# The projections' weight tiles loaded from ScalarE's queue instead of the sync engine's

## The chip, the cores and the metric

One Trainium2 chip; the kernel runs on 1 core. The metric is the device time of a run in microseconds (us). The kernel before has a median of 1959.77 us over 3 runs (1958.41 to 1960.76). The execution that was profiled took 1963.19 us, with a span of 1961.4 us from the first to the last instruction of the program.

## The reference

One layer of a hybrid decoder, on 1024 tokens of width 1024, float32, with 16 learned tokens put in front:

```
proj = rmsnorm(h) @ w_in                       # 1024 -> 10256 columns, split in 12 parts
q, k, v = silu(causal conv, 4 taps, of gq, gk, gv);  q, k normalised per head
o_a = gated delta rule over 8 heads of 128, in chunks (a triangular solve in each chunk)
o_b = retention over 4 heads of 256, in chunks, on rotated rq, rk and on rv
y = sigmoid(gate_a) * rms(o_a) * silu(gz) + sigmoid(gate_b) * silu(rg) * rms(o_b)
h = h + y @ w_out
h = h + (silu(a) * b) @ w_down,   a, b = split(causal conv, 3 taps, of rmsnorm(h) @ w_up)
out = rmsnorm(h), without the 16 tokens
```

## The kernel before

**Number format.** Each large product is made of three passes. An operand x is kept as x_hi (rounded to the matmul's fast format) and x_lo = x - x_hi, and the product is w_hi·x_hi + w_hi·x_lo + w_lo·x_hi.

**Tiles and units.** The first projection is made from 80 weight tiles of 1024 x 128 (tile t = 0 to 79; 512 KB each). Each tile is worked off in three *units* (t, 0), (t, 1), (t, 2): one third of the columns of the sequence, 24 matmuls into one PSUM bank. Units are numbered u = 3t + j and alternate between PSUM banks 0 and 1. The eight tiles of `w_out` (80 to 87) and the first six of `w_up` follow; the rest of the feed-forward block uses another scheme of tiles.

**What happens to a weight tile.** (1) A DMA loads it to the staging buffer `w_raw` (a few tiles go to a part of `ext`). (2) ScalarE (ACT) copies `w_raw` to `w_hi` (`split_high`, L1549). (3) VectorE (DVE) computes `w_lo = w_raw - w_hi` (`split_low`, L1936) and raises the semaphore `w_lo`. (4) TensorE (PE) uses both. `w_raw` is one buffer, so that the DMA of tile t+2 can only be issued when step 3 of tile t+1 is done. `w_hi` and `w_lo` have two buffers each, used by tiles in turn.

**What happens to a unit.** PE raises `units_done`. ACT copies the PSUM bank to the buffer `raw` (L1624, called the *evacuation* of the unit below) and raises `evac`. Unit u starts only when `evac` has reached u-1, that is when unit u-2, which used the same bank, has been evacuated (L1170: `pe.wait_ge(evac, ... u - 1)`).

**The order of work.** `front_plan()` makes one list of steps. Each engine's program walks the whole list and issues, for each step, its own part; an engine works strictly in that order, and waits on semaphores where a step needs another engine. The order in which an engine meets the steps is thus the order of the plan. The steps that matter here, in the order around a unit (t, 0):

- `("proj", t, 0)`: PE's 24 matmuls; on ACT the evacuation of that unit.
- `("split", t+1)`: `w_hi` of tile t+1 on ACT, `w_lo` of it on DVE.
- `("load", t+2)`: the DMA of tile t+2 into `w_raw`. Its wait is for `w_lo` of tile t+1. (In the stretch of the retention value tiles 24 to 31, a table `loads_at` places the loads one by one.) There are 79 of these steps, for tiles 3 to 81.
- `("proj", t, 1)`: the next unit, and its evacuation on ACT.

Between them the plan puts the steps of the recurrent parts: `conv` (L2044, L2048 on DVE) and `silu` (L1683 on ACT) for the delta rule's q, k, v tiles; `r_sc`, `r_out`, `r_ss` for a chunk of the retention (`r_ss`: Ln and Exp on ACT at L1696 and L1698, then the scaled output on DVE at L2103, which PE's next `r_out` at L1258 needs, since it reuses the banks); `dec`, `dec_e` (two Exp on ACT, L1723 and L1725), `qk` (L2168 on DVE, L2666 on GpSimd) for a chunk of the delta rule. Functions of ACT of different kinds need another table (`ACT_TABLE_LOAD`, L1533).

**The queues.** The sync engine (SP) issues nearly all DMAs of the kernel, in plan order: weight loads, stores of the rotated and convolved tiles to scratch in HBM (`store`, L806; `store_turned`, L813 and L815), and the loads of the chunks. ACT issues none before the change. GpSimd (POOL) issues the sums of the down projection's weights: four DMAs of 2816 KB at the end of tile 4, and small ones later. The loads from tile 82 on are issued by SP at L1034.

Of the kernel before, what the change touches and what calls it, by code (L numbers as in the profile page):

```python
# [60 lines left out]
T_ROT, T_K, T_RV, T_Q, T_V, T_ZB, T_ZA, T_END = 0, 16, 24, 32, 40, 48, 64, 80  # L61
# [357 lines left out]
def program(nc, io, sc, out):  # L419

    with ExitStack() as ctx:
# [10 lines left out]
        def sem(name):  # L432
            return ctx.enter_context(nc.semaphore("f1_" + name))
# [97 lines left out]
        def erow(at, n=1024):  # L531
            return tile8(ext[:, at:at + n])
# [4 lines left out]
        def wr(t):  # L537
            return (erow(4096) if t in (1, T_RV, T_RV + 2) else erow(5120) if t in (2, T_RV + 1) else w_raw[:, :, :])

        def w_seen(t):  # L540
            if t in (1, T_RV, T_RV + 2):
                return w_in[1], 16 * (1, T_RV, T_RV + 2).index(t) + 16
            if t in (2, T_RV + 1):
                return w_in[2], 16 * (2, T_RV + 1).index(t) + 16
            return w_in[0], 16 * (1 if t == 0 else t - 1 if t < T_RV else t - 4)

        def w_parts(t):
# [43 lines left out]
        w_hi, w_lo, units_done, evac, pe_x15 = (sem(n) for n in (  # L591
            "w_hi", "w_lo", "units_done", "evac", "pe_x15"))
# [139 lines left out]
        def weights_of(t):  # L732
            if t in (T_RV + 4, T_RV + 5):

                return io["w_in"][T_RV + 4 + t % 2]
            return io["w_in"][t] if t < T_END else io["w_out"][t - T_END] if t < T_UP else io["w_up"][t - T_UP]
# [62 lines left out]
        def _(sp):  # L799
# [22 lines left out]
            for step in plan:  # L822
                kind, a = step[0], step[1:]
                if kind == "intro":
# [15 lines left out]
                    sp.dma_start(sc["kt"][0, 0:PAD, :], zero[0:PAD, :]).then_inc(zero_done, 16)  # L840
                    for n in ("rvt", "rkt"):
                        sp.dma_start(sc[n][0, 0:PAD, :], zero[0:PAD, :]).then_inc(zero_done, 16)
                elif kind == "load":
                    t = a[0]
                    sp.wait_ge(w_lo, 1 if t == 3 else 3 if t in (T_RV, T_RV + 1) else T_RV + 1 if t == T_RV + 2 else
                               T_RV if t == T_RV + 3 else t)
                    sp.dma_start(wr(t), weights_of(t)).then_inc(w_seen(t)[0], 16)
                elif kind == "rope":
                    i = a[0]
                    store(0, S_RQ + 2 * i, d_rope, 6 * i + 4)  # L850
# [18 lines left out]
                elif kind == "silu":  # L869
                    t = a[0]  # L870
# [657 lines left out]
        def _(act):  # L1528
# [28 lines left out]
            for step in plan:  # L1557
                kind, a = step[0], step[1:]
# [33 lines left out]
                elif kind == "proj":  # L1592
                    t, j = a
# [31 lines left out]
                elif kind == "proj3":  # L1625
                    t = a[0]
# [20 lines left out]
                elif kind == "ab":  # L1647
                    table(LNEXP)
                    turned = psum[:, 7, 0:NCH * 2 * GH].rearrange("p (c g) -> p c g", c=NCH)
                    if a[0] == 0:  # L1650
                        act.wait_ge(ab_step, 1)
                        act.activation(gtmp[:, :, GH:2 * GH], turned[:, :, GH:2 * GH], ACT.Exp,
                                       scale=-1.0).then_inc(ab_step, 1)
                        act.activation(gabs[:, :, :], gtmp[:, :, 0:GH], ACT.Abs).then_inc(ab_step, 1)
                        act.wait_ge(ab_step, 3)
                        act.activation(gabs[:, :, :], gabs[:, :, :], ACT.Exp, scale=-1.0).then_inc(ab_step, 1)
                        act.wait_ge(ab_step, 4)
                        act.activation(gabs[:, :, :], gabs[:, :, :], ACT.Ln, bias=1.0).then_inc(ab_step, 1)
                        act.activation(rate[:, :], arow[:, 0, :], ACT.Exp).then_inc(ab_step, 1)
                    elif a[0] == 1:  # L1660
                        act.wait_ge(ab_step, 14)
                        act.activation(gates[:, :, NBEG], gcum[:, :].rearrange("p (c g) -> p c g", c=NCH),
                                       ACT.Exp).then_inc(ab_step, 1)
                        act.activation(gates[:, :, EGL], psum[:, 7, 216:288].rearrange("p (c g) -> p c g", c=NCH),
                                       ACT.Exp).then_inc(ab_step, 1)
                        act.activation(gates[:, :, KDEC], gates[:, :, KDEC], ACT.Exp).then_inc(ab_step, 1)
                    else:
                        act.wait_ge(pe_ab, 3)
                        act.activation(grows[:, :], psum[0:NCH * GH, 7, 288:416], ACT.Copy).then_inc(rows_out, 1)
                elif kind == "silu":  # L1670
                    t = a[0]
                    q = convs_before(t)
# [1094 lines left out]
```

## Time and profile before

| | |
|---|---|
| median of 3 runs | 1959.77 us |
| profiled execution, its span | 1963.19 us, 1961.4 us |
| PE busy | 1932.7 us (99%) |
| DVE busy | 1286.9 us (66%) |
| ACT busy | 795.8 us (41%) |
| POOL busy | 330.5 us (17%) |
| DMA, mean rate | 161 GB/s |

The profile page shows one execution. Busy time is that of computing instructions; issuing a DMA does not count as busy. In a timeline each row is an instruction (or several of one kind in a row): start, duration, engine, source line, operation, output <- inputs, shape, count, and in brackets the idle time of the engine before it with what ended it. SPq is the sync engine's own stream, in which the row of a DMA is only its issue.

### The profile page before, as it was taken

To read this page: it belongs to the slowest core of one execution; us is meant where nothing else is said; L and a number is where in the kernel's file an instruction comes from. 1 tells how busy PE (TensorE), PEld (TensorE's weight loads), DVE (VectorE), ACT (ScalarE), POOL (GpSimd) and SP (SyncE) were. 2 spreads that over 40 slices of the span, in tenths; PEclk is the share of its full clock that TensorE was granted. 3 is DMA by queue.
4 is the path that set the end of the run, shared out by engine and by line. 5 is a ranking of instruction groups with operands and counts; after the bars stand their busy time and mean duration, and the time that the engine had idled before them with its cause. 6 is when DMAs were issued, how large, how long until landed. Compare 5 with 4: busy or idle time off the path is not lost.

```text
span 1961.4 us, 32138 instructions
## 1 busy us (share of the span) xinstructions
PE 1932.7 (99%) x13173; PEld 1865.5 (95%) x13173; DVE 1286.9 (66%) x1612; ACT 795.8 (41%) x1094; POOL 330.5 (17%) x327
## 2 busy tenths in 40 slices
PE   8999999999999999999999999999999999999998
PEld 7999997999999999999999999999999999988887
DVE  6456764747676766676643333379988889866666
ACT  5223432534333444444443333334444444445443
POOL 0000002566573122222101101200000000000001
PEclk9999999999999999999999999999999999999999
DMA  9666567654555676555445642322433545577564
GB/s 293 219 206 140 129 168 189 200 174 152 171 184 140 155 201 171 160 143 170 147 119 171 177 122 82 100 84 63 132 88 117 152 151 162 153 254 264 191 191 161
DMA packets 301222, 315.99 MB, mean 161 GB/s; under 512 B 151004, under 2 KB 221124, under 8 KB 300948
## 3 DMA queue, kind: packets, MB, share of 16 engines
q1 hardware_dynamic: 291860, 290.86, 48.0%
q0 software_dynamic: 9216, 23.07, 5.9%
q8 instruction: 105, 1.72, 0.4%
q14 instruction: 41, 0.34, 0.1%
HBM read 222.76 MB, written 114.18 MB: 172 GB/s over the span
## 4 chain that ended last, share of the span: by engine, by line
PE 91%; DVE 4%; DMA 2%; ACT 1%; issue 1%; POOL 1%; SPq 0%; DVEq 0%; ACTq 0%; POOLq 0%
PE a_psum L1174 36%; PE a_psum L1469 18%; PE a_psum L155 10%; PE a_psum L1479 10%; PE a_psum L1161 5%; PE a_psum L1261 1%; PE a_psum L1280 1%; PE a_psum L1258 1%; PE a_psum L1366 1%; PE a_psum L1290 1%; PE a_psum L1350 1%; PE a_psum L1306 1%; PE a_psum L1381 1%; PE a_psum L1243 1%; PE a_psum L1389 1%
## 5 line engine op out<-in xcount | busy, mean ns | idle before, releaser
L1174 PE MATMUL a_psum<-xh,w_hi 128*128 128x342 f32 (+3 forms) x1632 | 528.6, 324 | 3.6 <-DVE w_lo L1936 3.6
L1174 PE MATMUL a_psum<-xl,w_hi 128*128 128x342 f32 (+3 forms) x1632 | 523.3, 321 | 0.0
L1174 PE MATMUL a_psum<-xh,w_lo 128*128 128x342 f32 (+3 forms) x1632 | 521.4, 319 | 0.0
L1174 PEld LDWEIGHTS a_psum<-xh,w_hi 128*128 128x128 f32 x1632 | 307.2, 188 | 6.2 <-DVE w_lo L1936 4.2
L1174 PEld LDWEIGHTS a_psum<-xl,w_hi 128*128 128x128 f32 x1632 | 307.4, 188 | 0.8
L1174 PEld LDWEIGHTS a_psum<-xh,w_lo 128*128 128x128 f32 x1632 | 307.1, 188 | 0.0
L1624 ACT ACTIVATE post<-a_psum 128x342 f32<-128x342 f32 (+3 forms) x204 | 93.1, 457 | 488.7 <-PE a_psum L1174 461.4
L1936 DVE TENSOR_TENSOR w_lo<-w_raw,w_hi 128x1024 fp32r<-128x1024 f32 x86 | 112.8, 1312 | 132.7 <-ACT w_hi L1549 132.7
L1549 ACT ACTIVATE w_hi<-w_raw 128x1024 fp32r<-128x1024 f32 x86 | 90.5, 1053 | 102.0 <-PE a_psum L155 74.7
L1479 PE MATMUL a_psum<-act_hi,down_hi 128*128 128x512 f32 (+1 forms) x324 | 124.0, 383 | 2.8 <-DVE act_lo L2477 2.7
L1469 PE MATMUL a_psum<-x_t_hi,up_hi 128*128 128x258 f32 x608 | 123.3, 284 | 2.7 <-DVE post L2424 2.5
L1479 PE MATMUL a_psum<-act_hi,down_lo 128*128 128x512 f32 (+1 forms) x324 | 124.2, 383 | 0.0
L1479 PE MATMUL a_psum<-act_lo,down_hi 128*128 128x512 f32 (+1 forms) x324 | 123.9, 382 | 0.0
L1469 PE MATMUL a_psum<-x_part_lo,up_hi 128*128 128x258 f32 x608 | 122.7, 283 | 0.0
L2356 DVE SCALAR_TENSOR_TENSOR post<-post,c_par,post 128x1024 f32<-128x1024 f32 x88 | 111.2, 1282 | 2.4 <-ACT post L1823 0.6
L2048 DVE SCALAR_TENSOR_TENSOR post<-post,a_par,post 128x1040 f32<-128x1040 f32 x72 | 97.0, 1347 | 2.6
L1469 PEld LDWEIGHTS a_psum<-x_t_hi,up_hi 128*128 128x128 f32 x608 | 95.0, 191 | 3.2 <-issue 2.9
L1469 PEld LDWEIGHTS a_psum<-x_part_lo,up_hi 128*128 128x128 f32 x608 | 94.0, 189 | 0.0
L2576 POOL DMA_DIRECT2D down_sums<-down_sums x22 | 17.9, 814 | 449.7 <-DVE post L2362 449.7
L1469 PE MATMUL a_psum<-x_t_lo,up_hi 128*128 128x258 f32 x456 | 92.8, 285 | 0.0
L1469 PE MATMUL a_psum<-x_b_hi,up_hi 128*128 128x258 f32 x456 | 91.8, 283 | 0.5 <-DVE u_three L2422 0.5
L1469 PE MATMUL a_psum<-x_t_hi,up_sum_lo 128*128 128x258 f32 x456 | 92.0, 283 | 0.0
(294 smaller groups left out, 3964.4 us busy)
## 6 DMA issues: line engine op xcount, KB each, us to landing
w_raw<-in_w_in SPq DMA_DIRECT2D x75, 512.0 KB, 3.9
up_raw<-in_w_up SPq DMA_DIRECT2D x19, 1024.0 KB, 4.9
mix_scratch<-post SPq DMA_DIRECT2D x32, 522.0 KB, 2.9
down_sums<-in_w_ffn_down POOLq DMA_DIRECT2D x4, 2816.0 KB, 31.1
act_scratch<-post SPq DMA_DIRECT2D x22, 512.0 KB, 2.7
down_raw<-down_sums SPq DMA_DIRECT2D x44, 256.0 KB, 2.7
act_raw<-act_sums SPq DMA_DIRECT2D x44, 256.0 KB, 3.1
ext<-mix_scratch SPq DMA_DIRECT2D x9, 1024.0 KB, 7.3
```

Source lines behind the costliest of these rows:

```text
L155: mm = pe.matmul(psum[:, bank + j, 0:n], w[:, k, :], x[:, k, col + n * j:col + n * j + n], start=(k == 0 and part == 0), stop=(k == KC - 1 ...
L1161: mm = pe.matmul(psum[0:rows_, u % 2, n * i:n * i + n], x[:, k, x0:x0 + rows_], w, start=(k == 0 and part == 0), stop=(k == KC - 1 and par ...
L1174: mm = pe.matmul(psum[:, u % 2, 0:n], w[:, k, :], x[:, k, at0:at0 + n], start=(k == 0 and part == 0), stop=(k == KC - 1 and part == 2))
L1243: mm = pe.matmul(four(7)[:, h, seen(c)], r_in[:, 8 + 2 * h + e, :], r_in[:, 2 * h + e, seen(c)], start=(e == 0), stop=(e == 1))
L1258: mm = pe.matmul(o, rvs[c % 2][:, n, :], rsc[:, h, seen(c)], start=True, stop=(c == 0))
L1469: mm = pe.matmul(region(i, n)[:, b, :], w[:, k, :], x[:, k, HP * b:HP * b + HP], start=(n < 4 and k == 0 and part == 0), stop=(k == 3 and ...
L1479: mm = pe.matmul(psum[:, (0, 4, 0, 4, 0, 4, 0)[p] + m, c0:c0 + n], a, b[:, c0:c0 + n], start=(p not in (2, 5, 6) and k == 0 and part == 0) ...
L1549: act.activation(w_parts(t)[0], wr(t), ACT.Copy).then_inc(w_hi, 1)
L1624: act.activation(dst, src, ACT.Copy).then_inc(evac, 1)
L1936: dve.tensor_tensor(lo, wr(t), hi.bitcast(F32), ALU.subtract).then_inc(w_lo, 1)
L2048: dve.scalar_tensor_tensor(out=acc[:, 0:n], in0=x, scalar=w, in1=acc[:, 0:n], op0=ALU.mult, op1=ALU.add).then_inc(d_conv, 1)
L2356: dve.scalar_tensor_tensor(out=acc_of(j, s), in0=u_out[s][:, c0:c0 + SEQ], scalar=par2[:, at0:at0 + 1], in1=acc_of(j, s), op0=ALU.mult, op ...
```

## The change

The branch for the step `load` is taken out of SP's program and put into ACT's, word for word except for the engine: the same plan, the same wait, the same source, destination and semaphore. The 79 loads of tiles 3 to 81 are thus issued by ACT; tiles 0 to 2 and those from 82 on stay with SP.

```
@@ sync engine @@
-                elif kind == "load":
-                    t = a[0]
-                    sp.wait_ge(w_lo, 1 if t == 3 else 3 if t in (T_RV, T_RV + 1) else T_RV + 1 if t == T_RV + 2 else
-                               T_RV if t == T_RV + 3 else t)
-                    sp.dma_start(wr(t), weights_of(t)).then_inc(w_seen(t)[0], 16)
@@ ScalarE @@
+                elif kind == "load":
+                    t = a[0]
+                    act.wait_ge(w_lo, 1 if t == 3 else 3 if t in (T_RV, T_RV + 1) else T_RV + 1 if t == T_RV + 2 else
+                                T_RV if t == T_RV + 3 else t)
+                    act.dma_start(wr(t), weights_of(t)).then_inc(w_seen(t)[0], 16)
```

## Rows read from the trace of the kernel before

**Rows 1.** The page's first part: busy time, share and instructions of each engine.
```profile
PE 1932.7 (99%) x13173; PEld 1865.5 (95%) x13173; DVE 1286.9 (66%) x1612; ACT 795.8 (41%) x1094; POOL 330.5 (17%) x327
```

**Rows 2.** Waits of PE: who waited for whom, us in total, times, longest.
```profile
PE a_psum L1174 <- DVE w_lo L1936: 3.6, 2, 2.1
```

**Rows 3.** Waits of the sync engine's stream, same columns.
```profile
SPq L847 <- DVE w_lo L1936: 311.7, 53, 15.0
```

**Rows 4.** Tile `w_raw`: durations min/median/max in ns; the page's POOL DMAs (mean 814 ns).
```profile
L847 SPq DMA_DIRECT2D w_raw<-in_w_in x74: 328/333/1416, 35.6 to 1152.5; - x74
DMA to landing us min/median/max: 3.4/3.9/12.8
...
L2576 POOL DMA_DIRECT2D down_sums<-down_sums x22 | 17.9, 814 | 449.7 <-DVE post L2362 449.7
```

**Rows 5.** Timeline of ACT and DVE, 1048 to 1053 us, a regular stretch.
```profile
1048.06 0.46 ACT L1624 ACTIVATE post<-a_psum 128x342 f32<-128x342 f32 x1 [1.26 <-PE a_psum L1174]
...
1051.83 0.46 ACT L1624 ACTIVATE post<-a_psum 128x342 f32<-128x342 f32 x1 [2.36 <-PE a_psum L1174]
...
1050.95 1.22 DVE L1936 TENSOR_TENSOR w_lo<-w_raw,w_hi 128x1024 fp32r<-128x1024 f32 x1
```

**Rows 6.** Timeline of ACT, DVE and PE, 646 to 653 us.
```profile
646.16 1.07 ACT L1683 ACTIVATE post<-post 128x1040 f32<-128x1040 f32 x1 [3.00 <-DVE post L2048]
...
649.27 0.63 ACT L1698 ACTIVATE y<-y 128x512 f32<-128x512 f32 x1
...
646.04 1.22 DVE L1936 TENSOR_TENSOR w_lo<-w_raw,w_hi 128x1024 fp32r<-128x1024 f32 x1
...
649.93 1.22 DVE L2103 TENSOR_TENSOR y<-a_psum,y 128x1024 f32<-128x1024 f32 x1 [0.88 <-ACT y L1698]
...
652.36 0.38 PE L1258 MATMUL a_psum<-ext,y 128*128 128x128 f32 x2
```

**Rows 7.** Timeline of ACT, DVE and PE, 686 to 697 us.
```profile
686.85 0.46 ACT L1624 ACTIVATE post<-a_psum 128x346 f32<-128x346 f32 x1 [0.70 <-PE a_psum L1174]
687.33 1.28 ACT L1533 ACT_TABLE_LOAD   x1
691.51 1.07 ACT L1683 ACTIVATE post<-post 128x1040 f32<-128x1040 f32 x1 [2.90 <-DVE post L2048]
...
696.01 0.44 ACT L1624 ACTIVATE post<-a_psum 128x346 f32<-128x346 f32 x1
...
691.39 1.22 DVE L1936 TENSOR_TENSOR w_lo<-w_raw,w_hi 128x1024 fp32r<-128x1024 f32 x1
...
692.66 0.43 PE L1174 MATMUL a_psum<-xh,w_hi 128*128 128x342 f32 x1 [2.06 <-DVE w_lo L1936]
...
696.55 0.37 PE L1174 MATMUL a_psum<-xh,w_hi 128*128 128x342 f32 x1
```

**Rows 8.** Timeline of ACT, DVE and POOL, 673 to 687 us.
```profile
673.63 0.46 ACT L1624 ACTIVATE post<-a_psum 128x346 f32<-128x346 f32 x1 [2.40 <-PE a_psum L1174]
...
679.00 1.06 ACT L1723 ACTIVATE y<-y 128x1024 f32<-128x1024 f32 x1 [1.23 <-DVE y L2158]
...
674.32 1.22 DVE L1936 TENSOR_TENSOR w_lo<-w_raw,w_hi 128x1024 fp32r<-128x1024 f32 x1
...
681.36 1.29 DVE L2168 TENSOR_TENSOR y<-a_psum,y 128x512 f32<-128x512 f32 x2 [1.13 <-ACT y L1725]
...
684.05 3.41 DVE L2044 TENSOR_SCALAR post<-post,a_par 128x1040 f32<-128x1040 f32 x1
...
684.05 2.39 POOL L2666 TENSOR_TENSOR y<-y 128x1024 f32<-128x1024 f32 x1 [0.17 <-POOL post L2662]
```

**Rows 9.** Timeline of ACT and PE, 104 to 107 us; the page's DMA issues.
```profile
104.01 1.06 ACT L1549 ACTIVATE w_hi<-w_raw 128x1024 fp32r<-128x1024 f32 x1 [6.20 <-DMA w_raw<-in_w_in]
...
106.38 0.43 PE L1174 MATMUL a_psum<-xh,w_hi 128*128 128x348 f32 x1 [1.52 <-DVE w_lo L1936]
...
down_sums<-in_w_ffn_down POOLq DMA_DIRECT2D x4, 2816.0 KB, 31.1
```

## Prediction

> **What bounds the kernel now.** I read the page's busy times first: PE computes for 1932.7 us of 1961.4 [rows 1]. The kernel is as long as PE's own work plus 28.7 us in which PE stands still, so a change of queue can only act on when PE stands still. Second, PE's waits: of its standing only 3.6 us, in two waits, is ended by a weight tile (the `w_lo` made at L1936) [rows 2]. That is nearly all a better way of loading the same tiles could give back. Third, the sync engine's stream: in 53 of the 79 loads it stands at L847 until DVE has made `w_lo`, 311.7 us together and up to 15.0 at once [rows 3]. This waiting is a part of the kernel's data dependence (one staging buffer), not of the queue. Today an engine with nothing to compute bears it. After the change ACT bears it, and behind a waiting load ACT holds the evacuation of PE's units, the silu and exponentials of the recurrent parts, and the next `w_hi`.
>
> **How much ACT may be late.** In a regular stretch the evacuations start 3.77 us apart (1048.06, 1051.83) and take 0.46 [rows 5]. PE needs a unit's evacuation only one unit later, so an evacuation may be late by 3.77 - 0.46 - 0.05 = some 3.2 us before PE stands. Longer units, and scan products between units, give more.
>
> **The regular places cost nothing.** The new load on ACT stands right behind ACT's `w_hi`. At best ACT waits for DVE's 1.22 us, then issues. The issue takes 333 ns on SP (median) [rows 4]; on ACT the trace shows none, and I bound it below by 0 (issued beside the array's work) and above by 0.81 us, the mean of POOL's DMA instruction [rows 4], and take 0.35, as the same kind of transfer does on SP. In the stretch of rows 5 `w_lo` ends at 1052.17; the load is issued by 1052.52, and the evacuation moves from 1051.83 to there, 0.7 us late. That is inside 3.2: cost 0. The last dozen loads look alike, alternately 0 and 0.7-0.8 late. I went through all 79, comparing the end of the awaited L1936 with the row that follows on ACT: about half put nothing off, most of the rest 0.2 to 3 us. If the 3.2 us of cover were not there, each would cost PE its lateness.
>
> **Place A, the load of tile 46 (646 us).** DVE makes `w_lo` of tile 45 only at 646.04 to 647.26, behind a convolution [rows 6]. In the kernel before, ACT had evacuated unit (44, 1) long before and waited 3.00 us for the silu's input. Now that evacuation stands behind the load: issued at 647.6, evacuated at 648.1. Then follows what ran from 646.16 to 649.90 without a gap (silu, table, Ln, Exp), 3.74 us: ends at 651.8 instead of 649.9. DVE's L2103, which waited for that Exp, runs 651.9 to 653.15, and PE's L1258 at 652.36 is the next `r_out`, which waits for it [rows 6]. Cost: 653.2 - 652.4 = 0.8 us.
>
> **Place B, the load of tile 49 (687 us).** `w_lo` of tile 48 ends at 692.61 and the evacuation behind the load moves from 686.85 to 692.96. After it come the table load (1.28), to 694.7, and the block that ran without a gap from 691.51 to 696.45 (silu, table, two Exp, the evacuation of (47, 2)), 4.94 us: it ends at 699.65. In the kernel before, the 2.90 us that ACT waited for DVE's convolution hid most of this; now the load's wait has used up that gap. PE's unit (48, 1) starts at 696.55 and needs that evacuation [rows 7]. Cost: 3.1 us, the largest single term.
>
> **Place C, the load of tile 48 (674 us).** `w_lo` of tile 47 ends at 675.54, the evacuation that started at 673.63 moves to 675.9, 2.3 late; 1.23 of this goes in ACT's gap before the Exp at 679.00, and 1.1 reaches DVE's L2168 at 681.36 [rows 8]. From there DVE is full up to the `w_lo` for which PE already stands at 692.66 [rows 7]. Cost up to 1.1. But L2044 at 684.05 took 3.41 us, ends just after POOL's L2666 (684.05 to 686.44), and its kind is short elsewhere: it may have been held by POOL, and then it would absorb the delay [rows 8]. Bounds 0 and 1.1; I take 0.6.
>
> **Place D, tiles 8 and 9 (91 to 107 us).** The DMA of tile 8 is the slowest, 12.8 us to landing against a median of 3.9 [rows 4], under POOL's four transfers of 2816 KB and behind two SP stores; ACT waits 6.20 us for it and PE then 1.52 [rows 9]. If it lands as before, the load of tile 9 makes ACT wait for `w_lo` up to 106.34, the evacuation of (7, 1) ends at 106.34 + 0.35 + 0.46 = 107.15, and PE starts at 107.2 instead of 106.38: +0.8. If it lands 1.5 us sooner, because the stores are no longer ahead of it in its queue, PE does not stand at all: -1.5. I take -0.8, in the nearer half to the gain, since only the two stores, not POOL's transfers, get out of the way.
>
> By the Trainium skill ("DMA: Bandwidth & Descriptors", "Queues, rings and completion order") each DMA engine takes turns between the queue rows it has work for, and SP and ACT have a row each; by that rule the load of tile 8 is no longer behind the stores and place D is the full -1.5. The same page ("Issuing engines are not separate DMA queues") says that issuing from several engines saves only sequencer time, "which is usually small relative to the DMA itself"; by that, place D keeps +0.8. The trace of before has no ACT queue and does not decide between them.
>
> **The other places.** Some ten more loads make an evacuation 2.5 to 5 us late. Most stand where scan products or longer units widen the cover. At two or three of them I find 0.1 to 0.4 us by the same reckoning; 0.7 for all, bounds 0 and 1.5.
>
> **What SP gains.** Its stores and chunk loads are no longer behind the 311.7 us of waits. Beside the two of rows 2, no wait of PE in the stretch of these loads is ended by a transfer, so an earlier load or store has nothing to shorten: 0. From tile 82 on nothing changes: 0.
>
> **Sum.** A 0.8 + B 3.1 + C 0.6 + D -0.8 + others 0.7 = 4.4; an ACT issue somewhat longer than SP's when both engines issue at once (SP's own reach 1.4 us [rows 4]) adds 0.1 at each of four places: 4.8. The profiled execution would go from a span of 1961.4 to 1966.2 and from 1963.19 to 1968.0. That execution lies 3.4 above the median of the runs; on the median the forecast is 1959.77 + 4.8 = 1964.6. The lowest sum of the bounds is 0.8 + 3.1 + 0 - 1.5 + 0 = 2.4, the highest 0.8 + 3.1 + 1.1 + 0.8 + 1.5 + 0.4 = 7.7.
>
> **Rivals.**
> - *The waits stay under cover.* ACT's chain at places A and B shifts with DVE's order (a convolution that starts a little sooner or later moves `w_lo` by as much), and the gain at D comes in full. For it: at A the excess is only 0.8, and every such place depends on the accidental order in 10 us. Against it: B is over by 3.1, and DVE is full there. It gives -1.5 to +3.5, say 1961.5. This is the case on the other side, not slower by what can be told: its place is B, its price is nothing, and it holds when `w_lo` of tile 48 is made 3 us sooner against ACT's chain.
> - *The weights come sooner, faster kernel.* Both waits for `w_lo` go, -3.6 [rows 2], 1956.2. Against it: the second (692.66) waits for DVE's order, not for a transfer [rows 7].
> - *The issue is dear on ACT.* At POOL's 0.81 us instead of 0.35, each of the four places costs 0.46 more (1.8), and evacuations now 2.5 to 3.2 late come over the edge, of which I count some four at 0.4 (1.6): 4.8 + 3.4 = 8.2, 1968.0. For it: SP's rows up to 1.4. Against it: the median of 333 ns.
> - *The change does nothing it says.* The loads will be issued elsewhere with certainty; no chance given.
>
> **Chances.** Forecast (2.4 to 7.7) 0.56; under cover 0.28; dear issue or landings slower by a microsecond 0.13; faster 0.03. What a measurement of this kernel can tell from no change is about 0.2%, 3.9 us. Slower by more: four fifths of the forecast's case, 0.45, with 0.13 of the dear one: 0.58. Faster by more: 0.03, as even the full 3.6 does not reach it without help. Within: 0.39. The range 1960.0 to 1970.5 leaves out the faster case, a part of the covered one, and the far end of the dear one.
>
> **What would show it.** In the profile after: rows of L1665-1669 on ACT's stream as DMA issues of about 0.33 us; ACT's waits with `w_lo` as releaser near 300 us less than SP had (what ACT spends computing falls out); SP's L847 gone; near 652, 692 and 697 us PE rows with idle time released by ACT L1624 or DVE L2103, together some 4.5 us; at 106 us either no PE wait or one of over 2 us; PE busy unchanged at 1932.7. The prediction is wrong if PE's idle before 1187 us doesn't grow, if the growth lies in the regular stretch after 1040 us (then the cover is not 3.2), or if the loads' median landing moves from 3.9 by more than 0.5.

## The result, and the profile after

The changed kernel's median is 1964.27 us over 19 runs against 1960.44 for the kernel before over 19; the ratio is 1.0019, with a 95% interval of 1.0013 to 1.0025. It is slower by 3.8 us, 2.5 to 4.9 by the interval. Measured once more (e12 below) it is 1.0021 (1.0012 to 1.0030). Of the 19 runs of the changed kernel one took 10885 us and is left out of the ratio; the other 18 lie between 1962.3 and 1967.0. The ratios in this document are those on record for each comparison. They are not the quotients of the two medians beside them, and an effect in us is the ratio's.

Here are the busy times of the changed kernel and some of its waits of PE, which answer to [rows 1] and [rows 2] (who waited for whom: us in total, times, longest):

```profile
PE 1933.3 (99%) x13173; PEld 1865.6 (95%) x13173; DVE 1281.3 (65%) x1612; ACT 795.7 (41%) x1094; POOL 330.7 (17%) x327
```

```profile
PE a_psum L1169 <- ACT post L1619: 4.5, 3, 2.1
...
PE a_psum L1253 <- issue: 0.4, 1, 0.4
...
PE a_psum L1337 <- ACT ext L1729: 0.2, 1, 0.2
```

PE computes for as long as before. The two waits for a weight tile are gone; in their place PE waits three times for ACT's evacuation. In the profile PE stands still for 14.9 us of the first 1187, against 13.6 before (14.0 in the second profile of the change). ACT's own waits say why: it now stands 33 times in front of an evacuation until DVE has made `w_lo`, where SP stood before [rows 3].

```profile
ACT post L1619 <- DVE w_lo L1936: 127.9, 33, 8.8
```

The tile `w_raw` answers to [rows 4]: the issue on ACT takes what it took on SP, and the median landing is 3.8 us against 3.9; only the slowest went from 12.8 to 10.3.

```profile
L1669 ACTq DMA_DIRECT2D w_raw<-in_w_in x74: 334/334/1129, 36.8 to 1154.4; - x74
...
DMA to landing us min/median/max: 3.3/3.8/10.3
```

The regular stretch, as [rows 5]. The load is issued at 1054.18, right after `w_lo`; the evacuation behind it is some 0.7 us late, and PE does not notice:

```profile
1050.04 0.46 ACT L1619 ACTIVATE post<-a_psum 128x342 f32<-128x342 f32 x1 [1.26 <-PE a_psum L1169]
...
1054.18 0.33 ACTq L1669 DMA_DIRECT2D w_raw<-in_w_in  x1
1054.57 0.46 ACT L1619 ACTIVATE post<-a_psum 128x342 f32<-128x342 f32 x1 [3.12 <-DVE w_lo L1936]
```

Place A (tile 46), as [rows 6]. The load keeps ACT until 645.4, so that the silu can start only at 645.76, behind the evacuation; the Exp ends at 649.49, and L2103 waits 2.74 us for it where it waited 0.88:

```profile
645.02 0.33 ACTq L1669 DMA_DIRECT2D w_raw<-in_w_in  x1
645.40 0.46 ACT L1619 ACTIVATE post<-a_psum 128x346 f32<-128x346 f32 x1 [8.80 <-DVE w_lo L1936]
...
648.86 0.63 ACT L1698 ACTIVATE y<-y 128x512 f32<-128x512 f32 x1
...
649.52 1.23 DVE L2103 TENSOR_TENSOR y<-a_psum,y 128x1024 f32<-128x1024 f32 x1 [2.74 <-ACT y L1698]
...
650.96 0.46 PE L1253 MATMUL a_psum<-ext,y 128*128 128x128 f32 x2 [0.38 <-issue]
```

Places C and B (tiles 48 and 49), as [rows 7, 8]. PE stands at 682, 692 and 698 us, and each time ACT's evacuation ends it. The last two belong to the load of tile 49. The first does not come from the change: e2 below, which leaves these three loads with SP, has it too.

```profile
674.25 0.37 ACTq L1669 DMA_DIRECT2D w_raw<-in_w_in  x1
674.67 0.46 ACT L1619 ACTIVATE post<-a_psum 128x346 f32<-128x346 f32 x1 [4.76 <-DVE w_lo L1936]
...
689.90 1.22 DVE L1936 TENSOR_TENSOR w_lo<-w_raw,w_hi 128x1024 fp32r<-128x1024 f32 x1
691.14 0.33 ACTq L1669 DMA_DIRECT2D w_raw<-in_w_in  x1
691.52 0.46 ACT L1619 ACTIVATE post<-a_psum 128x346 f32<-128x346 f32 x1 [8.16 <-DVE w_lo L1936]
...
697.60 0.44 ACT L1619 ACTIVATE post<-a_psum 128x346 f32<-128x346 f32 x1
...
682.12 0.43 PE L1169 MATMUL a_psum<-xh,w_hi 128*128 128x346 f32 x1 [0.44 <-ACT post L1619]
...
692.13 0.40 PE L1169 MATMUL a_psum<-xh,w_hi 128*128 128x342 f32 x1 [2.15 <-ACT post L1619]
...
698.09 0.43 PE L1169 MATMUL a_psum<-xh,w_hi 128*128 128x342 f32 x1 [1.94 <-ACT post L1619]
```

The same wait of e2, where tiles 46, 48 and 49 are loaded by SP:

```profile
681.16 0.43 PE L1179 MATMUL a_psum<-xh,w_hi 128*128 128x346 f32 x1 [0.46 <-ACT post L1629]
```

Place D (tiles 8 and 9), as [rows 9]. The DMA of tile 8 landed early enough; PE starts unit (8, 0) at 104.37 without a wait:

```profile
99.62 1.06 ACT L1544 ACTIVATE w_hi<-w_raw 128x1024 fp32r<-128x1024 f32 x1 [2.13 <-DMA w_raw<-in_w_in]
...
104.37 0.32 PE L1169 MATMUL a_psum<-xh,w_hi 128*128 128x348 f32 x1
```

**One table for all runs.** As the order of PE's instructions is the same in every kernel here, I took the start of the same instruction in each profile, less its start in the profile of before: the table is in us, and a step from one column to the next is what a kernel lost (or gained) between the two marks. The marks are (start of unit (8, 0); of (44, 0); of unit (47, 0), behind A; of (48, 0), behind C; of (48, 1), behind B; of (49, 0); of (55, 0), behind the opening of the delta scan; the last unit of tile 79).

```
                       8,0   44,0   47,0   48,0   48,1   49,0   55,0   79,2
after                -2.0   -2.0   -1.3   -0.5   +1.5   +1.6   +1.6   +2.0
e12_after_again      -2.1   -1.9   -1.3   -0.3   +1.8   +1.9   +1.9   +2.3
e1_wait_only         -2.2   -1.0   -0.2   +0.5   +2.6   +2.6   +2.6   +2.6
e2_tile8             -2.2   -2.3   -2.3   -2.5   -2.5   -2.5   -1.8   -1.8
e3_early             -1.8   -1.9   -1.9   -2.2   -2.2   -2.2   -2.2   -2.2
e4_three             -0.2   -0.2   +1.1   +2.0   +4.1   +4.1   +4.1   +4.1
e5_only_49           -2.1   -1.8   -1.8   -0.5   +2.2   +2.2   +2.2   +2.2
e6_all_but_three     -2.1   -2.2   -2.2   -2.3   -2.3   -2.3   +3.5   +3.9
e7_halves            +0.6   +3.2   +4.3   +5.9   +8.0   +8.0   +8.0   +9.0
e8_below_46          -2.3   -2.1   -2.1   -2.1   -2.2   -2.2   -2.0   -2.0
e9_from_50           -1.8   -1.9   -1.9   -2.3   -2.4   -2.3   -1.9   -1.5
e10_50_51            -1.7   -1.6   -1.6   -1.9   -1.9   -1.9   +4.8   +4.8
e11_all_but_three_   -1.7   -1.5   -1.5   -1.7   -1.7   -1.7   -1.7   -1.3
```

The changed kernel's profile is only 2.0 us behind that of before at the last mark, and 1.2 at the end of the kernel. That execution of before was a long one (1963.19 against a median of 1960.44): it holds the wait at 106 us. Of the other five profiles with tile 8 on SP only e4's holds it in full. Against the kernels that leave A, B and C alone and do not have the loss at 722 us described below (e2, e3, e8: -1.8 to -2.2), the changed kernel is some 4 us behind, as its times say.

### The profile page after: what moved, and what is told of

It is laid out like the page before. It is cut to its first block, busy times and chain, and to the rows that moved or that the text cites. A ratio compares the mean times of both kernels' runs of the same rounds, so it can differ in the third digit from the quotient of the medians.

```text
span 1962.6 us, 32138 instructions
## 1 busy us (share of the span) xinstructions
PE 1933.3 (99%) x13173; PEld 1865.6 (95%) x13173; DVE 1281.3 (65%) x1612; ACT 795.7 (41%) x1094; POOL 330.7 (17%) x327
## 4 chain that ended last, share of the span: by engine, by line
PE 91%; DVE 4%; DMA 2%; ACT 1%; issue 1%; POOL 1%; SPq 0%; DVEq 0%; ACTq 0%; POOLq 0%
PE a_psum L1169 37%; PE a_psum L1464 18%; PE a_psum L155 10%; PE a_psum L1474 10%; PE a_psum L1156 5%; PE a_psum L1256 1%; PE a_psum L1275 1%; PE a_psum L1253 1%; PE a_psum L1361 1%; PE a_psum L1285 1%; PE a_psum L1345 1%; PE a_psum L1301 1%; PE a_psum L1376 1%; PE a_psum L1238 1%; PE a_psum L1384 1%
## 5 line engine op out<-in xcount | busy, mean ns | idle before, releaser
L1544 ACT ACTIVATE w_hi<-w_raw 128x1024 fp32r<-128x1024 f32 x86 | 90.6, 1053 | 91.4 <-PE a_psum L155 65.6
```

Source lines behind the costliest of these rows:

```text
L1544: act.activation(w_parts(t)[0], wr(t), ACT.Copy).then_inc(w_hi, 1)
```

## The experiments

My theory after the result: the cost is ACT's waiting at A, B and C, the gain is tile 8's DMA out of SP's queue. The rivals: the issue instruction on ACT, or a cost spread over all 79 loads. Most kernels differ from the changed one in which tiles ACT loads. They have both branches, with a condition (the comments list the conditions of the different runs):

```
+def on_act(t):
+    return t == 8          # e2;  e3: t < T_RV (24);  e4: t in (46, 48, 49);  e5: t == 49
+                           # e6, e11: t not in (46, 48, 49);  e8: t < 46;  e9: t >= 50;  e10: t in (50, 51)
...
-                elif kind == "load":                              # on SP
+                elif kind == "load" and not on_act(a[0]):
...
+                elif kind == "load" and on_act(a[0]):             # on ACT, as in the change
```

**e1, the wait alone.** SP's branch is that of before; ACT gets the branch without its DMA:

```
+                elif kind == "load":
+                    t = a[0]
+                    act.wait_ge(w_lo, 1 if t == 3 else 3 if t in (T_RV, T_RV + 1) else T_RV + 1 if t == T_RV + 2 else
+                                T_RV if t == T_RV + 3 else t)
```

> SP issues all 79 loads as before; ACT at the same places of the plan waits for the same w_lo and issues nothing. Theory (the cost is ACT's waiting, the gain is tile 8's DMA out of SP's queue): the losses of the changed kernel near 651, 682, 697 and 852 us stay (0.6 + 0.8 + 2.1 + 0.4, a little less since no 0.33 us issue stands behind the wait), the gain of 1.8 us at 106 us is gone and tile 8 lands after about 12.8 us again: +4 to +6 us against before. Rival 1 (the cost is the issue instruction on ACT, not the wait): about 0. Rival 2 (the cost is contention of two DMA rows): about 0.

Measured: 1965.46 against 1961.67, ratio 1.0020 (1.0011 to 1.0030). With no DMA on ACT at all, the cost is the whole one, within the interval. Both rivals fall. The steps stand at the same places (A +0.8, +0.7 up to (48, 0) and +2.1 behind it in the table). One more step, +1.1 by unit (9, 0), has no counterpart in the change: tile 9 landed in 10.3 us, ACT's wait for its `w_lo` lasted until 116.3, and PE stood 1.0 us for the evacuation behind it. The part on tile 8 did not hold: with its load on SP it landed in 10.5 us here, and PE did not wait at 106.

**e2, tile 8 alone**; **e3, tiles 3 to 23**.

> Only the load of tile 8 is issued by ACT, the other 78 by SP as before. Theory: its DMA, issued at about 91 us as before, no longer stands behind the two stores of SP (issued 87.5 and 90.1), lands in some 9 us instead of 12.8, and PE's wait of 1.5 us at 106 us goes: -1.5 to -1.8 us. Rival (the landing of tile 8 came from the loads before it being earlier, or from all loads being off SP): 0 to -0.3 us, landing stays above 12.

> The loads of tiles 3 to 23 (rotary and key tiles, to about 270 us) are issued by ACT, the rest by SP. Theory: the gain at 106 us is all there is in this stretch, ACT's evacuations are late by less than the cover: -1.5 to -2.0 us. Rival (each ACT issue or wait costs a little everywhere): 21 loads at a quarter of the whole cost, so +0.5 to +1.5 us on top of the gain, about -0.5.

Measured: 1960.53 and 1961.20 against 1961.67, ratios 0.9995 (0.9986 to 1.0003) and 0.9993 (0.9984 to 1.0002). In the profiles PE does not wait at 106, as expected. In the times no gain can be told from zero (-1.0 us, -2.7 to +0.6, and -1.4, -3.1 to +0.4), and they decide neither for the theory nor for the rivals. The DMA issued at 90 to 92 us (size, us to landing), on SP in e1, before and e4, then on ACT in e2 and e3:

```profile
w_raw<-in_w_in SPq DMA_DIRECT2D x1, 512.0 KB, 10.5
```

```profile
w_raw<-in_w_in SPq DMA_DIRECT2D x1, 512.0 KB, 12.8
```

```profile
w_raw<-in_w_in SPq DMA_DIRECT2D x1, 512.0 KB, 13.2
```

```profile
w_raw<-in_w_in ACTq DMA_DIRECT2D x1, 512.0 KB, 8.7
```

```profile
w_raw<-in_w_in ACTq DMA_DIRECT2D x1, 512.0 KB, 8.5
```

Over all profiles: on SP 12.8, 10.5, 13.2, 11.4, 10.3, 10.1; on ACT as one DMA 8.7, 8.7, 8.5, 8.5, 8.6, 9.3, 9.1. So the transfer does land earlier from ACT's queue, by some 2.5 us in the mean. The load before it, at 77 us, has no stores just ahead of it: it landed in 9.3 to 10.8 us from SP (7 profiles) and in 9.4 to 10.7 from ACT (6), without a difference. But PE waits its 1.5 us or more at 106 only where tile 8 takes over 12, in two of the six (at 11.4 some 0.3 is lost). By these six profiles, which are few, I estimate the gain of the change there at 0.5 us in the mean. That e3 costs nothing that can be told also agrees with the cover: its 21 loads put evacuations off by up to 2.5 us, and none of them makes PE wait. Where the cover ends, at 3.2 or elsewhere, no run shows.

**e4, tiles 46, 48 and 49**; **e5, tile 49 alone**.

> Only the loads of tiles 46, 48 and 49 are issued by ACT. Theory: these three carry nearly the whole cost (0.6 at 651, 0.8 at 682, 2.1 at 697 us): +3.0 to +4.0 us, PE idle released by ACT's evacuation L1624 near 682 and 697 us. Rival (the cost is spread over the 79 loads): under +0.5 us.

> Only the load of tile 49 is issued by ACT. Theory (ACT's gap of 2.9 us before the silu at 691.5 is used up by the wait, and the block of 4.9 us behind it ends late): PE's unit (48, 1) starts 2 to 3 us later, released by ACT's evacuation, and the kernel is +2 to +3 us. Rival (the cost at 697 us needs the delays of tiles 46 and 48 before it): under +1 us.

Measured: e4 1965.83 against 1961.67, ratio 1.0021 (1.0012 to 1.0031), the whole cost by three of 79 loads. e5 1962.67 against 1959.57, ratio 1.0013 (1.0005 to 1.0022), 2.6 us. Both theories hold, and both rivals fall, that of e5 by a narrow margin in the times (its interval begins at 1.0 us) and clearly in the profile. The load of tile 49 alone makes the steps at (48, 0) and at (48, 1), so nothing there needs tile 48's. In the profile of e5 the loss from (47, 0) to (48, 1) is 4.0, more than the 3.1 of the change: around the end of PE's wait the granted clock fell. First PE's row, then windows of 692.7 to 695 and 695 to 698 us (length; busy and count of PE, PEld, DVE, ACT, POOL; granted clock, DMA share, GB/s) of e5, then of the changed kernel:

```profile
692.18 0.62 PE L1179 MATMUL a_psum<-xh,w_hi 128*128 128x342 f32 x1 [3.36 <-ACT post L1629]
```

```profile
692.70:695.00 2.30, 2.30 (x10) 2.30 (x9) 2.00 (x3) 2.27 (x3) 0.00 (x0) 0.50 0.81 256
695.00:698.00 3.00, 3.00 (x12) 3.00 (x11) 0.00 (x0) 2.99 (x5) 2.11 (x2) 0.50 0.87 142
```

```profile
692.70:695.00 2.30, 2.30 (x16) 2.30 (x16) 2.30 (x2) 2.27 (x3) 2.02 (x1) 1.00 0.96 274
```

At 0.50 (1.2 GHz) PE made 10 matmuls in 2.3 us, at 1.00 (2.4 GHz) 16. In the changed kernel unit (48, 0) ran at 1.00 and PE then waited 1.94 at (48, 1) for the same evacuation; in its second profile it ran at 0.50 and waited 0.41. The end is nearly the same, as ACT's block sets it; in e5 the slow unit went on past the block.

**e6, all but those three.**

> All loads on ACT but those of tiles 46, 48 and 49, which stay with SP. Theory: the cost of 3.5 to 4 us goes, the gain at 106 us stays: -1 to -1.8 us against before, 5 us below the changed kernel, with 76 of 79 loads still issued by ACT. Rival (cost spread over all loads): +2 us or more.

Measured: 1966.20 against 1959.57, ratio 1.0026 (1.0011 to 1.0041), on 12 runs from 1959.0 to 1971.4. The theory missed. The rival's number (+2 or more) was met, but not its cause: the cost is not spread. The profile has no loss at A, B or C, and one at a new place, PE waiting 4.0 us at 722.6 to 726.6:

```profile
726.57 2.64 PE L1371 MATMUL a_psum<-ext 128*128 128x128 f32 x15 [3.97 <-DVE ext L2240]
```

So the theory was not complete: I asked which loads do this.

**e8, tiles below 46**; **e9, tiles from 50**; **e10, tiles 50 and 51**; **e11, the kernel of e6 again**.

> The loads of tiles 3 to 45 are issued by ACT, the rest by SP. The run before (all but tiles 46, 48, 49 on ACT) was 5 us slower instead of 1 us faster; its profile shows PE waiting 4.0 us at 722 to 727 us for DVE's first scaled v chunk (L2240), behind a late o_b chunk. Theory (that loss comes from the loads of tiles 50 and on being on ACT, whose waits stand in the opening of the delta scan): here it is absent, only the gain at 106 us stays: -1 to -1.8 us. Rival (it comes from PE being early at 700 us through the gain at 106): it is there too, +2 to +5.

> The loads of tiles 50 to 81 are issued by ACT, the rest by SP. Theory: the loss at 722 us appears in a part of the runs, and some 0.3 at 851 us: +1 to +6 us, with a wide spread from run to run. Rival: only the 0.3 at 851 us, +0 to +0.5.

> Only the loads of tiles 50 and 51 are issued by ACT. Theory: these two stand at the opening of the delta scan, and give the loss at 722 us by themselves: +1 to +5 us, wide spread. Rival (the loss needs more of the loads, or the loads of tiles 52 and on): under 0.5 us.

> The kernel with all loads on ACT but those of tiles 46, 48 and 49, once more. If the place at 722 us is one of chance within a run (a landing and a collision of DVE and POOL), its times fall again into a group near 1959 and one near 1965 to 1971, and the profile shows a PE wait at 722 us if its execution is of the slow group, none if of the fast one. Rival (something on that chip): one group, 1 us below before.

Measured against 1960.38:

- e8: 1960.54, ratio 1.0004 (0.9995 to 1.0013).
- e9: 1966.15, ratio 1.0025 (1.0013 to 1.0038); its 8 runs are 1959.3, 1959.7 and then 1964.4 to 1969.6.
- e10: 1963.21, ratio 1.0015 (1.0005 to 1.0025), runs from 1958.5 to 1969.1.
- e11: 1961.07, ratio 1.0009 (0.9998 to 1.0021), seven runs from 1959.3 to 1962.3 and four from 1965.4 to 1967.8.

The loads of tiles 50 and 51 on ACT are enough, and the loss comes in a part of the executions. The theories of e9, e10 and e11 hold. Of e8's only the absence of the loss does: the gain of 1 us or more can't be seen (+0.8 us, -1.0 to +2.5). Its rival falls, since PE has no wait at 722 us in its profile. A single long run is no proof, as the kernel before has one of 1966.0 among its 31; what tells is that six of e9's eight are long.

The two kinds of profile, DVE and POOL at 720 to 728 us: first e10, with the loss, then e9, whose profiled execution does not have it:

```profile
722.56 1.23 DVE L2306 TENSOR_TENSOR post<-post,post 128x1026 f32<-128x1026 f32 x1 [3.38 <-DMA post<-ob_scratch]
723.71 3.43 DVE L2240 TENSOR_TENSOR ext<-y,gates 128x512 f32<-128x512 f32 x2
...
723.16 2.83 POOL L2676 TENSOR_TENSOR y<-y 128x1024 f32<-128x1024 f32 x1 [14.67 <-PE a_psum L1311]
```

```profile
720.24 1.23 DVE L2306 TENSOR_TENSOR post<-post,post 128x1026 f32<-128x1026 f32 x1 [1.50 <-DMA post<-ob_scratch]
721.39 1.28 DVE L2240 TENSOR_TENSOR ext<-y,gates 128x512 f32<-128x512 f32 x2
...
722.73 3.33 POOL L2676 TENSOR_TENSOR y<-y 128x1024 f32<-128x1024 f32 x1 [14.69 <-PE a_psum L1311]
```

L2240 is a pair of 0.69 us instructions. In e9 the first starts before POOL's L2676 and takes 0.68 us; in e6 and e10 it starts 0.3 and 0.5 us after it and lasts 2.83 us, until 0.55 us after POOL's end. What decides is a margin of one to two microseconds: DVE stands behind a chunk of o_b that SP loads at 716, and in both profiles with the loss (e6, e10) that DMA landed in 5.5 and 6.1 us against 4.3 to 4.7 in all others. That the loads of tiles 50 and 51 on ACT bring this about is shown by the times of e8, e9 and e10; by which transfer they delay it is not.

**e7, each load as two DMAs.**

```
-                    act.dma_start(wr(t), weights_of(t)).then_inc(w_seen(t)[0], 16)
+                    for n in range(2):
+                        act.dma_start(wr(t)[:, 4 * n:4 * n + 4, :], weights_of(t)[:, 4 * n:4 * n + 4, :]).then_inc(w_seen(t)[0], 16)
```

(the counts that ACT waits for are adapted).

> The changed kernel with each of ACT's 79 loads issued as two DMAs of 256 KB: one more issue of about 0.33 us on ACT behind each wait. Theory (only the few places without cover pay): the doubled issue adds about 0.35 us at each of the four or five places, +1.5 to +2.5 us against the changed kernel, +5 to +6 against before. Rival (issues don't hold ACT's computing): the same as the changed kernel, +3.8. Rival (each issue costs PE something everywhere): 79 x 0.35 = +28 us.

Measured: 1974.58 against 1959.57, ratio 1.0064 (1.0052 to 1.0076), +12.6 us, on 5 runs of 1969.9 to 1974.9; the profiled one was the shortest. All three expectations missed. The issue does hold ACT, and more dearly than I had it: the issues have a median of 450 ns, up to 1.45 us, and two pairs in the regular stretch took 0.82 and 0.98. The table has +2.6 by (8, 0) against the changed kernel (the second half landed in 11.1 us, so PE waits at place D), +1.2 at (9, 0), +1.4 at unit (24, 0), and 0.5 to 0.8 more than the change at each of A, unit (48, 0) and the place at 851 us. It is not the test of one more issue that I meant it to be, since halves land later too.

**e12, the changed kernel again.**

> The changed kernel once more. In six profiles with the load of tile 8 on SP it landed in 10.1 to 13.2 us, and PE waited at 106 us only where it took over 12; on ACT it landed in 8.5 to 9.3. Theory (PE is held at 651, 697 and 851 us by ACT's waits for tiles 46, 49 and 58 in every execution, and is so late at 697 that DVE and POOL don't collide at 723): PE waits at 697 again about 2 us, released by ACT's evacuation, none over 0.5 at 724, +3 to +5 us against before. Rival (the collision at 723 is part of the changed kernel's cost): a PE wait of some 4 us at 724.

Measured: 1964.77 against 1960.79, ratio 1.0021 (1.0012 to 1.0030). PE's waits at 682, 692 and 698 us are there again (0.65, 2.18 and 0.41, the last after a unit at half the clock), none at 724: DVE's L2230 starts at 724.1, POOL's L2666 at 726.9. PE, on whose products POOL waits, comes so late out of place B that the collision does not take place. The theory holds, and the rival falls for this execution. As in the first profile of the change, the wait at 682 is not the change's.

## Why the prediction was right or wrong

The forecast was 1964.6, slower by 4.8; measured 1964.27, slower by 3.8 (2.5 to 4.9). The mechanism was right: ACT bears SP's wait, and PE pays at A and B. The ratio of 1.0019 stands right at the bound of 0.2% by which I split "slower" (0.58) from "within" (0.39), and by its point value it is on the side to which I gave less. Step by step:

- *SP's wait becomes ACT's.* Right, shown by e1: the wait without any DMA gives 1.0020, the change 1.0019. Before an evacuation ACT stands 127.9 us for `w_lo`, where SP stood 311.7.
- *A cover of 3.2 us, regular places at 0.* The regular places are right: e3 and e8 put 21 and 43 loads on ACT for 0.9993 and 1.0004, and none of PE's new waits lies in the stretch after 1040 us. The cover holds up to the 2.5 us of e3; its end is not shown.
- *A at 0.8.* Measured from (44, 0) to (47, 0): +0.6 in both profiles of the change, +0.8 in e1 and +1.3 in e4.
- *B at 3.1.* Right, and by its own path. From the end of `w_lo` of tile 48 to the start of unit (48, 1) it is 3.9 us before and 7.0 in both profiles of the change and in e4, 3.1 more; in e1, without the issue, 6.6. I had left out one step that the path contains: unit (48, 0) needs the evacuation of (47, 1), which comes only after `w_lo` and the issue. So 1.0 of the 3.1 stands already at (48, 0), which starts 1.0 us after `w_lo`'s end instead of 0.05.
- *C at 0.6.* This term was mis-sized: it is nothing, my lower bound. From the start of (47, 0) to the end of `w_lo` of tile 48 it is 13.7 us before, 13.5 and 13.7 in the change, 13.6 in e4, and 13.3 to 13.7 in the kernels that leave tile 48 with SP, but for e5 (14.0). The delay does not reach `w_lo`. (No run has tile 48 alone on ACT; e5 has the whole step without it.) In e1 the cushion that I had named is seen: DVE's second row at this place (L2044 in the kernel before) is held by POOL for 3.15 us instead of 3.41. In the change that row takes 1.76, but another one before it, L2161, takes 2.85 instead of 1.23, and this is not the load's doing either: all kernels but before, e1 and e5 have it so. The change, then e2, with tile 48 on SP:

```profile
677.78 2.85 DVE L2161 TENSOR_TENSOR y<-y,a_cst 128x1024 f32<-128x1024 f32 x1
...
684.21 1.76 DVE L2044 TENSOR_SCALAR post<-post,a_par 128x1040 f32<-128x1040 f32 x1
```

```profile
676.76 2.92 DVE L2171 TENSOR_TENSOR y<-y,a_cst 128x1024 f32<-128x1024 f32 x1
...
683.26 1.75 DVE L2054 TENSOR_SCALAR post<-post,a_par 128x1040 f32<-128x1040 f32 x1
```

- *D at -0.8.* The landing is earlier from ACT's queue in every profile, as I had reckoned for the gain. But the -1.7 us from unit (7, 2) to (8, 0) in the change's profile is no proof of it: e1, e5, e9 and e10, with tile 8 on SP, have -1.4 to -1.7 there too. The wait of [rows 9], which I took for a fixed part of the kernel, is in two of the six profiles with tile 8 on SP. How much it is worth in the times stays open: e2, e3 and e8 (0.9995, 0.9993, 1.0004) have intervals from -3.1 to +2.5 us.
- *Other places at 0.7, dear issue 0.4.* The profile has +0.4 around 851 us and +0.1 at tile 24. The issues on ACT have a median of 334 ns, and the 0.4 for a dearer one was not needed.
- *Nothing from SP's free queue.* Right in the two profiles of the changed kernel, but not safe: with the loads of tiles 50 and 51 on ACT and PE not held up at 697 us, the kernel loses 5 us in many executions. The forecast had no term for it, and in the change it is hidden by B, which makes PE late.

A 0.6, B 3.1, the others 0.5 and nothing for C are 4.2 without D, which fits 3.8. The forecast's 4.8 came as near as it did partly by luck: C, the others and the dear issue were 1.2 too much together, and A 0.2, against a gain of 0.8 at D for which the times show no certain value. Of the signs I named, PE's idle time before 1187 us does grow, but by 1.3 and 0.4 us in the two profiles, as before's profile has its own waits of 1.5 at 106 and 2.1 at 692; alone, this sign would have said little. The median landing moved from 3.9 to 3.8.

By the Trainium skill ("DMA: Bandwidth & Descriptors", "Queues, rings and completion order"), a DMA engine takes turns between the queue rows it has work for. The landings agree, 8.5 to 9.3 us from ACT's row against 10.1 to 13.2 behind two stores in SP's. The same page of the Trainium skill says in "Issuing engines are not separate DMA queues" that issuing from several engines saves only the sequencer's time. By these numbers that is too narrow here, where a transfer has others ahead of it in the same row.

No version here beats the kernel before: the best medians, e2 and e3, have intervals that hold 1.

## What to carry to other kernels

A DMA that has to wait for a semaphore costs its engine above all the wait (e1: the whole cost without any DMA). The issue comes on top, some 0.4 us at place B and more when it is doubled (e7). Move such a DMA only to an engine whose next instructions can stand still that long, and price each of the places, not the average: three of 79 carried the whole cost. But don't expect the cost to go when these places are mended. With the three loads back on SP (e6) the kernel was no faster in the comparison, since an engine that is no longer late met a collision elsewhere. And a single profile can hold a wait that most executions don't have: a second profile of the kernel before would have told it.

## What was not expected of the hardware

- The granted clock was 0.50 for over 3 us (6.6 in e5), from about the end of PE's wait near 692 to 699 us, in e1, e4, e5, e7 and e12; PE had waited 2.75, 2.16, 3.36, 2.74 and 2.18. It stayed at 1.00 in the kernel before and in the first profile of the change, where PE had waited 2.06 and 2.15. So the length of the wait alone does not tell these cases apart.
- A DVE instruction over 128x512 elements, 0.69 us by itself, lasted 2.83 us in e6 and e10, where it started inside POOL's L2676.
